# A third down-projection unit a chunk by seven block products in place of eight

## The reference, cut to what matters

```python
def swiglu(x, w_gate, w_up, w_down):
    return (jax.nn.silu(x @ w_gate) * (x @ w_up)) @ w_down        # D_FF = 2816
h = h + 0.5 * swiglu(rmsnorm(h, ffn1_norm[l]), ffn1_w_gate[l], ffn1_w_up[l], ffn1_w_down[l])
...
ff = jnp.square(jax.nn.relu(x @ w_ff1[l])) @ w_ff2[l]             # D_FF_2 = 4096
x = layer_norm(DEEPNORM_ALPHA * x + ff, ln2_g[l], ln2_b[l])
```

## Time and profile before

| | |
|---|---|
| median of 3 runs | 2044.6 us (2044.06 to 2045.38) |
| span of the profiled execution | 2042.5 us |
| TensorE busy | 2034.5 us |
| VectorE busy | 1389.1 us |
| ScalarE busy | 1018.4 us |
| POOL (GpSimd) busy | 92.8 us |

### The profile page before, as it was taken

The page is one execution under the profiler, slowest core; times in us unless marked ns, Lnnn a source line. Parts: engine busy times, 40 slices in busy tenths (PEclk is TensorE's granted clock), DMA queues, the critical chain, the costliest instruction groups (busy, mean ns, idle before and its releaser), DMA issues.

```text
span 2042.5 us, 25162 instructions
## 1 busy us (share of the span) xinstructions
PE 2034.5 (100%) x10364; PEld 1718.3 (84%) x10364; DVE 1389.1 (68%) x1624; ACT 1018.4 (50%) x1290; POOL 92.8 (5%) x133
## 2 busy tenths in 40 slices
PE   9999999999999999999999999999999999999998
PEld 7888888888888888888888888888888888888887
DVE  6655687775757566877675667757767677577675
ACT  6444576453445335775443365644444466445331
POOL 1001010000010001100100000000100000000000
PEclk9999999999999999999999999999999999999999
DMA  9655554465566656544656474555755656455552
GB/s 333 211 187 166 178 162 141 167 214 185 186 197 210 194 168 201 165 145 145 226 191 197 153 242 155 166 172 173 239 186 189 204 153 194 156 185 193 196 189 83
DMA packets 225569, 377.73 MB, mean 185 GB/s; under 512 B 6592, under 2 KB 113216, under 8 KB 225456
## 3 DMA queue, kind: packets, MB, share of 16 engines
q1 hardware_dynamic: 221472, 362.64, 54.1%
q0 software_dynamic: 3984, 13.49, 2.2%
HBM read 375.05 MB, written 1.05 MB: 184 GB/s over the span
## 4 chain that ended last, share of the span: by engine, by line
PE 98%; DVE 1%; ACT 0%; issue 0%; DVEq 0%; POOL 0%; ACTq 0%; POOLq 0%
PE pb L1656 63%; PE pb L1667 18%; PE pb L1670 9%; PE pb L1679 2%; PE pb L1725 1%; PE pb L1803 1%; DVE wl L2109 0%; PE pb L1802 0%; PE pb L1790 0%; PE pb L1860 0%; PE pb L1782 0%; PE pb L1645 0%; DVE lS L2292 0%; PE pb L1649 0%; PE pb L1647 0%; PE pb L1684 0%
## 5 line engine op out<-in xcount | busy, mean ns | idle before, releaser
L1891 ACT ACTIVATE wh<-raw 128x2048 fp32r<-128x2048 f32 (+2 forms) x347 | 654.2, 1886 | 626.6 <-PE pb L1656 271.3
L2109 DVE TENSOR_TENSOR wl<-raw,wh 128x2048 fp32r<-128x2048 f32 (+2 forms) x347 | 777.3, 2247 | 149.0 <-ACT wh L1891 147.8
L1656 PE MATMUL pb<-wh,x 128*128 128x512 f32 (+1 forms) x2144 | 651.3, 385 | 0.0
L1656 PEld LDWEIGHTS pb<-wh,x 128*128 128x128 f32 x2144 | 400.7, 188 | 77.9
L1656 PE MATMUL pb<-wl,x 128*128 128x512 f32 (+1 forms) x1072 | 421.1, 393 | 0.1
L1667 PE MATMUL pb<-x,wh 128*128 128x512 f32 x1568 | 397.0, 395 | 0.0
L1667 PEld LDWEIGHTS pb<-x,wh 128*128 128x128 f32 x1568 | 283.3, 189 | 51.8
L1656 PE MATMUL pb<-wl,mh 128*128 128x512 f32 (+1 forms) x740 | 255.7, 391 | 0.0
L1656 PE MATMUL pb<-wh,ml 128*128 128x512 f32 (+1 forms) x740 | 253.7, 388 | 0.0
L1656 PE MATMUL pb<-wh,mh 128*128 128x512 f32 (+1 forms) x740 | 253.5, 388 | 0.0
L1656 PEld LDWEIGHTS pb<-wl,x 128*128 128x128 f32 x1072 | 201.4, 188 | 42.2 <-issue 3.7
(11 more groups left out here) (365 smaller groups left out, 1611.8 us busy)
## 6 DMA issues: line engine op xcount, KB each, us to landing
raw<-in_w_in_dram SPq DMA_DIRECT2D x100, 1024.0 KB, 5.3
raw<-in_w_ff_dram SPq DMA_DIRECT2D x64, 1024.0 KB, 5.3
raw<-in_ffn_w_down_dram SPq DMA_DIRECT2D x44, 1024.0 KB, 4.9
raw<-in_ffn_w_up_dram SPq DMA_DIRECT2D x42, 1024.0 KB, 5.3
raw<-in_ffn_w_gate_dram SPq DMA_DIRECT2D x41, 1024.0 KB, 5.3
raw<-in_w_branch_dram SPq DMA_DIRECT2D x24, 1024.0 KB, 5.0
raw<-in_w_out_dram SPq DMA_DIRECT2D x16, 1024.0 KB, 5.0
raw<-in_w_in_dram SPq DMA_DIRECT2D x4, 832.0 KB, 4.4
```

Source lines behind the costliest of these rows:

```text
L1656: ins = e.matmul(pb[b][:, 0:c1 - c0], x[:, s, cols], w[:, n, c0:c1], start=(it["first"] and n == 0 and q == 0), stop=(it["stop"] and n == ...
L1891: e.activation(hi, raw, ACT.Copy).then_inc(m.high_done, 1)
L2109: e.tensor_tensor(lo, raw, hi.bitcast(F32), ALU.subtract).then_inc(m.low_done, 1)
```

## The change

In 25 down units (called seven units here) the 2 x 2 x 2 blocks are multiplied by seven products in place of eight: with A the hidden values (t by slot) and B the weights (slot by output half), sums of blocks are multiplied and the results recombined. They are units 2, 3, 4 of six in the first chunk of three gated FFNs, and in the second block's FFN units 2, 3, 4 of six in the first chunk, 0, 1, 2 of four in the second and 0, 1 of six in the third. Per seven unit the program gains these items, besides 21 matmuls (`seven`) in place of 24:
- in `low`, VectorE also makes four sums of weight blocks (`sum`, 4 x 512 columns) and leaves out one block of the rest; ScalarE rounds the sums (`sumhigh`), VectorE makes their rest (`sumlow`). There are two buffers for sums, so those of the third unit of a chunk go where the first one's were, and its `low` waits for the first one's matmuls. In the planner every `low` behind it is held as well until the first seven unit has been planned.
- POOL makes four differences of hidden blocks (`diff`, three operations of 256, 128, 128 columns) when the product is ready; ScalarE rounds them (`diffhigh`), VectorE makes the rest (`difflow`), each two ticks after the other. The seven unit waits for `difflow` before its first matmul.
- four of the seven products are summed over the chunk's seven units in the four side banks, three in main banks. After the last, `recombine` (one operation of ScalarE, eight of VectorE, 512 columns each) adds the side banks' sums to `h`.

In the second block the second group of 512 hidden rows is now made by wide units, so that the first group is two token units and not four. The mixer's constants are loaded later (`loads`), as their room is used by the new buffers.

The diff, cut to its core (new functions are shown whole; semaphore names, buffer addresses and ScalarE's and POOL's simple items are left out):

```diff
@@ advance
         while self.nlo < self.nhi:
-            self.add("low", j=self.nlo)
+            n = self.seven.get(self.nlo)
+            if n is not None and n > 1 and n - 2 not in self.sum_free:
+                break
+            self.add("low", j=self.nlo, n=n, after=self.sum_free.get(n - 2) if n is not None else None)
             self.nlo += 1
+            self.sum_low_next()
+            if n is not None:
+                self.sum_high_due = n
...
-            self.add("high", j=j, after=self.freed.get(j - NH))
+            self.add("high", j=j, after=self.freed.get(j - NH), n=self.seven.get(j))
             self.nhi += 1
+            self.sum_high_next()
+
+    def sum_high_next(self):
+        n, self.sum_high_due = self.sum_high_due, None
+        if n is not None:
+            self.add("sumhigh", n=n, after=self.sum_free.get(n - 2))
+            self.sum_low_due = n
+
+    def sum_low_next(self):
+        n, self.sum_low_due = self.sum_low_due, None
+        if n is not None:
+            self.add("sumlow", n=n)
@@ group
+            if job.get("seven"):
+                if t == 0:
+                    self.seven_products(j, job)
+                self.tick()
+                continue
...
+    def seven_products(self, j, job):
+        n, slots = self.next("seven"), job["slots"]
+        self.seven_of[j] = n
+        self.sum_high_next()
+        self.sum_low_next()
+        need = self.need("M", slots, [0, 1]) + self.need("D", [n], [0])
+        mains, first = [], []
+        for t, b in ((0, 0), (0, 1), (1, 0)):
+            first.append((t, b) not in self.opened)
+            if first[-1]:
+                self.main_use[t, b] = self.use(2 * t + b)
+                self.opened.add((t, b))
+            mains.append(self.main_use[t, b])
+        if job["seven"] == "first":
+            self.side_uses = [self.side() for _ in range(4)]
+            self.side_count = self.nside
+        assert self.side_count == self.nside
+        v = self.pe("seven", j=j, n=n, slots=slots, mains=mains, sides=self.side_uses, first=first,
+                    begin=job["seven"] == "first", end=job["end"], need=need)
+        self.freed[j] = self.sum_free[n] = v["p"]
+        for s in slots:
+            self.m_free[s] = v["p"]
+        if job["end"]:
+            r = self.next("recombined", 2)
+            self.add("recombine", p=v["p"], uses=self.side_uses, coef=job["coef"], n=r,
+                     need=self.h_ready[0] + self.h_ready[1])
@@ ffn1, ffn2
+            self.seven_units = () if opening or n0 else (2, 3, 4)
...
+            self.seven_units = {0: (2, 3, 4), 1536: (0, 1, 2), 2560: (0, 1)}[n0]
-            first = 2 if n0 == 0 else 0
+            first = 1 if n0 == 0 else 0
...
+    def differences(self, q, need):
+        n = self.next("diff")
+        assert n < 3 or n - 3 in self.sum_free
+        self.add("diff", q=q, n=n, need=need, after=self.sum_free.get(n - 3))
+        def high():
+            self.add("diffhigh", n=n, after=self.sum_free.get(n - 3))
+            self.later.append(low)
+        def low():
+            self.add("difflow", n=n)
+            self.ready["D", n, 0] = ("diff_low", n + 1)
+        self.later.append(lambda: self.later.append(high))
+        return ("diff_ready", n + 1)
@@ pe_program
+        elif k == "seven":
...
+            for x, y, k, (b, g), first, stop in (
+                    ([x[:, s0, T] for x in a], w, 0, q1, begin, it["end"]),
+                    ([x[:, s1, T] for x in a], w, 2, q2, b2, False),
+                    ([x[:, 3, :] for x in d], w, 3, q3, b3, False),
+                    ([x[:, 1, :] for x in d], v, 0, q5, begin, it["end"]),
+                    ([x[:, 0, :] for x in d], v, 1, q7, begin, it["end"]),
+                    ([x[:, 2, :] for x in d], v, 2, q6, begin, it["end"]),
+                    ([x[:, s1, U] for x in a], v, 3, q4, b4, False)):
+                if y is v:
+                    pe.wait_ge(m.sum_low, n + 1)
+                if first:
+                    pe.wait_ge(m.evac[b], g)
+                e.matmul(pb[b][:, :], x[0], y[1][:, k, :], start=first, stop=False)
+                e.matmul(pb[b][:, :], x[0], y[0][:, k, :], start=False, stop=False)
+                ins = e.matmul(pb[b][:, :], x[1], y[0][:, k, :], start=False, stop=stop)
@@ VectorE, low of a seven unit
+                B, V = raw.rearrange("p (a n) -> p a n", n=512), m.sum[n % 2]
+                v.pe(it["after"])
+                v.step(e.tensor_tensor(V[:, 0:2, :], B[:, 0:4:3, :], B[:, 1:2, :].broadcast_to([P, 2, 512]), ALU.add))
+                v.own_steps()
+                v.step(e.tensor_tensor(V[:, 2, :], V[:, 0, :], B[:, 3, :], ALU.add))
+                e.tensor_tensor(lo[:, 0:512], raw[:, 0:512], hi[:, 0:512].bitcast(F32), ALU.subtract)
+                v.own_steps()
+                e.tensor_tensor(V[:, 3, :], V[:, 2, :], B[:, 2, :], ALU.add).then_inc(m.sums_ready, 1)
+                e.tensor_tensor(lo[:, 1536:2048], raw[:, 1536:2048], hi[:, 1536:2048].bitcast(F32), ALU.subtract)
+                v.wait_ge(m.sums_ready, n + 1)
+                e.tensor_tensor(lo[:, 1024:1536], raw[:, 1024:1536], hi[:, 1024:1536].bitcast(F32),
+                                ALU.subtract).then_inc(m.low_done, 1)
```

More of the change, by code:

```diff
@@ L384, with __init__ @@
 class Plan:
-    def __init__(self, total):
+    def __init__(self, total, seven=None):
         self.total = total
+        self.seven, self.seven_of = seven or {}, {}
+        self.seven_units, self.seven_slots = (), {}
+        self.sum_high_due = self.sum_low_due = None
+        self.sum_free, self.opened = {}, set()
         self.items, self.units = [], []
@@ L671, in to_ln, with down @@
         return after
-    def down(self, name, l, k0, n_units, sizes, coef, after, end=False):
+    def down(self, name, l, k0, n_units, sizes, coef, after, end=False, loads=None):
         def epi(t, p, uses):
@@ L692, in cut, with seven @@
                 after(1, 1)
+        def seven(i):
+            return ("first" if i == min(self.seven_units) else "next") if i in self.seven_units else None
         u = 0
+        self.opened = set()
         for size in sizes:
-            first, last = u == 0, u + size == n_units
+            last = u + size == n_units
+            if last and loads:
+                loads()
             if last and after:
@@ L698, in down @@
                                  slots=[2 * u + 4 * i + k for k in range(4)], segs=[(b, 0, 512)],
-                                 first=first and i == 0, last=(i == size // 2 - 1),
+                                 first=None, last=(i == size // 2 - 1),
                                  epi=add_up if end and b else half_epi(b), sum=end and b == 1 and i == size // 2 - 2,
@@ L705, in down @@
                                  slots=[2 * (u + i), 2 * (u + i) + 1], segs=[(0, 0, 512), (1, 512, 1024)],
-                                 first=first and i == 0, last=last and i == size - 1, epi=epi)
+                                 first=None, last=last and i == size - 1, epi=epi, coef=coef,
+                                 seven=seven(u + i), end=u + i == max(self.seven_units, default=None))
                             for i in range(size)])
@@ L747, in ffn1 @@
                 c0 += n
-            self.down(dn, l, n0, sum(chunks) // 256, sizes, 0.5, after if n0 else None)
+            self.down(dn, l, n0, sum(chunks) // 256, sizes, 0.5, after if n0 else None, loads=loads if n0 else None)
     def silu_t(self, n, root):
@@ L863, in ffn2 @@
                                  slots=list(range(4 * i, 4 * i + 4)), segs=[(c, 0, 512)], first=(i == 0),
-                                 last=(i == 1), epi=self.relu_t(4 * c)) for c in range(2) for i in range(2)],
+                                 last=(i == 1), epi=self.relu_t(4 * c)) for c in range(first) for i in range(2)],
                            start=True)
@@ L870, in ffn2 @@
                     n_t += 1
-            self.down("w_ff2_2", l, n0, n_chunks * 2, sizes, 1.0, after if n0 == 2560 else None, n0 == 2560 and l == L - 1)
+            self.down("w_ff2_2", l, n0, n_chunks * 2, sizes, 1.0, after if n0 == 2560 else None, n0 == 2560 and l == L - 1,
+                      loads if n0 == 2560 else None)
     def start(self):
@@ L1461, in ready @@
             return
+        if isinstance(event, list):
+            self.all_ready(event)
+            return
         name, value = event
@@ L1604, in pool_program @@
             e.dma_start(m.wgu[:, :], m.A["wgu4"][l]).then_inc(m.wgu_landed, 16)
+        elif k == "diff":
+            n, D = it["n"], m.diff[it["n"] % 3]
+            M = m.mn[it["q"]][:, :].rearrange("p (a n) -> p a n", n=P)
+            po.ready(it["need"])
+            po.pe(it["after"])
+            po.step(e.tensor_tensor(D[:, 0:2, :], M[:, 0:2, :], M[:, 1:4:2, :], ALU.subtract))
+            po.own_steps()
+            po.step(e.tensor_tensor(D[:, 2, :], D[:, 0, :], M[:, 3, :], ALU.add))
+            po.own_steps()
```

(3 more changed lines are left out.)

107 lines of the change are left out of this document (90 added, 17 removed).

## The result

The changed kernel takes **2151.35 us** (median of four runs, 2150.65 to 2152.55), the kernel before 2044.67 us beside it (2044.06 to 2045.38): a ratio of **1.0522, 95% interval [1.0507, 1.0537]**. It is 5.2% slower; 2129 was predicted, with a range of 2050 to 2155. The profiled execution took 2152.55 us with a span of 2150.8.

A forecast was written before the change was run, and what follows sets the result against it. TensorE, busy for 2034.5 of 2042.5 us, was taken as the bound. From the 2044.6 median: less 17.0 for matmuls, plus 20.7 gated chunks, 68.2 second block, 12.6 clock, gives 2129 us; range 2050 to 2155.

The forecast's parts named there:

- Rival 1: Whole kernel: engine queues stall TensorE as worked out from the planned order; 2116 to 2153 us, 2129 likeliest; chance 0.70.
- Rival 2: Whole kernel: only the data chains count, splits ahead of `sumlow` and `difflow` being mostly done; 2060 us; chance 0.17.
- rival 3: Whole kernel: VectorE never decides, TensorE stays full and the kernel gets faster; 2028 us; chance 0.06.
- Rival 4: Clock falls at each of thirteen stalls and stays low longer than at the start; 2189 us; chance 0.07.
- The third unit: Third seven unit of five chunks: TensorE stalls 6.5 us for `sumlow`, queued behind held `low` items.
- Bank wait: Gated chunks, after the third seven unit: side banks come free late by `recombine`, 0.4 us each.
- A: Second block's first FFN chunk: 6.5 us at the third unit plus 3.3 for bank 0, 9.8 a layer.
- B: Second block's second FFN chunk: stalls of 4.2 and 9.5 us for `difflow`, 0.8 in the third unit; 14.5 a layer.
- C: Second block's third FFN chunk, two seven units: VectorE without pause frees banks late, 4.4 + 0.6 = 5.0 us a layer.
- First group: Head of second block's FFN, group half as long: less TensorE work covers VectorE's normalizing; 4.8 us more a layer.
- The clock: TensorE's lower clock after stalls: 1.4 us for each of nine over 6 us, 12.6 in all; ends 0 and 36.
- VectorE is not slowed: POOL's `diff` beside VectorE's splits: `diff` costs 1.7 to 7.6 us, VectorE keeps its pace; nothing added.

## Why the prediction was right, and which term was off

**The direction and the rival.** Rival 1 (the queues stall as worked out) is what happened. Its upper end, 2153, was reached almost in full; its lower end stands in the prediction as 2116 and as 2105, which decides nothing here. Rival 2's time (2060) and rival 3's (2028) are out; yet the 0.7 us that rival 2 gives the third unit is what is left there once the sums come first. Rival 4 had the clock at 5.6 us a stall; it is 1.7 to 3.1.

**The gain**, 17.0 us: 75 of 128x512 less. Shown by the gated chunks with two units: 4.1 worked out for 18 matmuls, 3.4 measured.

**The third unit**, 6.5 in five chunks: 6.37 to 6.42, with VectorE's list as it was written out. **Bank wait** behind it in gated chunks, 0.4: seen there once with 0.4 (and twice behind B with 0.47). **A**, 3.3 for bank 0: 3.06 and 2.87.

**B**: 4.2 for the first difference, 4.5 measured; 9.5 for the second, 9.6 measured; 0.8 in the third unit did not come. The rest of its difference was ready at 1588.18; at the full pace the second unit (4.77 us from 1582.71) would have been over at 1587.5, but it ran at the low clock at first and ended about 1590.1. VectorE before the second of these waits:
```profile
1573.20 1.22 DVE L2268 TENSOR_TENSOR sum<-raw 128x1024 f32<-128x1024 f32 x1 [7.37 <-PE pb L1796]
...
1577.48 4.49 DVE L2264 TENSOR_TENSOR wl<-raw,wh 128x2048 fp32r<-128x2048 f32 x2
1581.88 0.69 DVE L2284 TENSOR_TENSOR diffl<-diff,diffh 128x512 fp32r<-128x512 f32 x1
```
One operation of 0.6 us stands behind 7.4 us of idling for T and 8.7 us of other units' work.

**C**, 5.0: 3.33 + 1.07 = 4.40. **First group**, 4.8: 5.3. All waits: 87.0 us (87.8 less the 0.8 above), where the terms of the gated chunks and the second block (20.7 and 68.2) made 88.9. No wait term is off by more than 0.8 us.

**The clock is the term that was mis-sized**: 12.6 us taken, half of 2.8 for nine stalls, and **33 measured**, near the upper bound of 36. The halving assumed that a stall might not set the clock back, and left out those under 6 us; all 13 long waits did, the 3.3 us one of C too. The 2.8 us itself came from the kernel's start, where matmuls were slow while the profile of the kernel before has a granted clock of 1.00 (0.98 to 4.76 us); so that it came close to the cost behind a wait was not a given. With 33 in place of 12.6 the sum is 2149.5, 2 us under the measured time; that it comes so near is in part luck, as 5.1 us of the account are unexplained and the wait terms were 1.9 us too high. The rule of the Trainium skill that the prediction weighed (TensorE: Matmul & The Clock Gate, HAM oscillation: idle gaps send the engine back to half its clock) was borne out by the windows above, and it would have given 25 us.

**"VectorE is not slowed"** beside `diff` was wrong, at a small price. VectorE in B while GpSimd made a difference:
```profile
1548.26 1.38 DVE L2268 TENSOR_TENSOR sum<-raw 128x1024 f32<-128x1024 f32 x1
1549.68 0.83 DVE L2270 TENSOR_TENSOR sum<-sum,raw 128x512 f32<-128x512 f32 x1
1550.44 0.95 DVE L2271 TENSOR_TENSOR wl<-raw,wh 128x512 fp32r<-128x512 f32 x1
```
and GpSimd:
```profile
1548.64 1.32 POOL L1713 TENSOR_TENSOR diff<-diff,mn 128x128 f32<-128x128 f32 x1
1550.04 0.80 POOL L1715 TENSOR_TENSOR diff<-mn,diff 128x128 f32<-128x128 f32 x1
```
Without GpSimd beside them the three take 1.22, 0.69 and 0.68. That fits the row on SBUF interfaces in the Trainium skill (GPSIMD Engine Reference, 1. Specifications). Ahead of B's first wait such excesses add up to 1.0 us (1548 to 1561), more than the 0.3 that the 4.2 was short of; that they are its cause is argued, no run isolates it.

**What stays open**: 5.1 us of the account, why equal waits cost the clock 0, 1.7 or 3 us, and how much of the time a better order of VectorE's work would give back.

## What to carry to other kernels

A gain on the bound engine has to be set against the helper engine's *order* at each place, not its average load: 173 us of work fitted into VectorE's free time on average, and still one operation of 0.6 us came 9.6 us late because it stood behind a wait and other units' work. Ask first where the new work can sit without a hold and without standing ahead of an instruction that frees a bank: six of the 25 units passed that test and were worth 3.4 us; the other 19, with the shorter first group that came with them (about 15 us), cost 110.

An idle stretch of a full TensorE is paid for twice: 88 us of waits brought 33 us of slow matmuls with them. In all the kernels here every wait of 3.3 us or more lost 1.4 to 3.1 us in this way, so price such a wait with 2 to 3 us on top.

## What had not been expected of the hardware

- A wait of TensorE as short as 2.7 us was followed by a granted clock of 0.50 in 17 of 22 cases of one execution (1.5 to 3.1 us lost each), with the clock at 1.00 over the wait itself in both of the cases shown; waits of 2.87 and 3.06 us in the changed kernel lost nothing. Idle time of 5.6 us was followed by the low clock in 11 of 11 cases.
- GpSimd and VectorE slow each other. A 128x128 operation of GpSimd took 0.46 us at its fastest and up to 2.5 beside a whole low part of VectorE; VectorE's 512-column operation 0.95 in place of 0.68.
